# Placement in SBUF: the slots of the split-weight ring 128 bytes apart within a line of 512, other tensors moved, DMA scratch of 8 KB for 16 KB

## The reference, cut to what matters

```python
h = rms_norm(x, norm_mix)
proj, gates = h @ w_in                          # 3608 columns, then 3 x 2048 gate columns
y_a, y_b, y_c = swa(proj), stick_breaking(proj), nsa(proj)   # small attentions
merged = sum(sigmoid(g_i) * (y_i @ w_branch_i))
x = x + merged @ w_out
h = rms_norm(x, norm_ffn)
x = x + (silu(h @ w_gate) * (h @ w_up)) @ w_down
out = rms_norm(x, norm_final)
```

## Time and profile before

| | us |
|---|---|
| median of 3 runs | 1381.56 |
| fastest, slowest run | 1380.27, 1384.85 |
| span of the profiled execution (first to last instruction) | 1378.3 |
| TensorE busy, of that span | 1364.8 |
| VectorE busy | 922.5 |
| ScalarE busy | 702.5 |
| GpSimd busy | 46.2 |

### The profile page before, as it was taken

The page is one execution under the profiler, slowest core; times in us unless marked ns, Lnnn a source line. Parts: engine busy times, 40 slices in busy tenths (PEclk is TensorE's granted clock), DMA queues, the critical chain, the costliest instruction groups (busy, mean ns, idle before and its releaser), DMA issues.

```text
span 1378.3 us, 26427 instructions
## 1 busy us (share of the span) xinstructions
PE 1364.8 (99%) x11280; PEld 1332.1 (97%) x11280; DVE 922.5 (67%) x1189; ACT 702.5 (51%) x912; POOL 46.2 (3%) x70
## 2 busy tenths in 40 slices
PE   8999999999999999999999999999999999999997
PEld 8999999999999999999999999999999999999997
DVE  6455557667654657666788788875446788887554
ACT  7333356656545654465654555454334455545444
POOL 4000010000000110000000000000000000000111
PEclk9999999999999999999999999999999999999999
DMA  7777755455565767546556756566556665666653
GB/s 255 245 217 217 212 148 154 140 151 141 152 192 163 198 204 221 179 163 200 165 181 198 219 171 196 185 208 210 195 195 181 191 211 172 196 194 231 210 195 123
DMA packets 135264, 261.08 MB, mean 189 GB/s; under 512 B 8448, under 2 KB 25408, under 8 KB 134768
## 3 DMA queue, kind: packets, MB, share of 16 engines
q1 hardware_dynamic: 133328, 251.89, 59.8%
q0 software_dynamic: 1792, 7.57, 1.5%
q10 hardware_dynamic: 32, 0.01, 0.0%
HBM read 257.33 MB, written 2.10 MB: 188 GB/s over the span
## 4 chain that ended last, share of the span: by engine, by line
PE 89%; DVE 8%; ACT 1%; issue 1%; ACTq 0%; POOL 0%; DVEq 0%; POOLq 0%
PE bank L638 24%; PE bank L639 23%; PE bank L640 23%; PE bank L877 5%; PE bank L880 4%; PE bank L879 4%; PE bank L627 2%; DVE weight_lo_ring L1269 2%; DVE weight_sums_lo L1289 1%; DVE weight_sums L1278 1%; PE bank L776 1%; DVE act_rows L1329 1%; ACT weight_hi_ring L1039 1%; PE bank L687 1%; DVE raw_ring L1280 1%
## 5 line engine op out<-in xcount | busy, mean ns | idle before, releaser
L1269 DVE TENSOR_TENSOR weight_lo_ring<-raw_ring,weight_hi_ring 128x1024 fp32r<-128x1024 f32 (+2 forms) x480 | 581.0, 1220 | 317.0 <-ACT weight_hi_ring L1039 263.4
L1039 ACT ACTIVATE weight_hi_ring<-raw_ring 128x1024 fp32r<-128x1024 f32 (+2 forms) x432 | 449.1, 1052 | 348.6 <-PE bank L640 281.1
L638 PE MATMUL bank<-weight_hi_ring,hT_hi 128*128 128x256 f32 (+2 forms) x1280 | 384.5, 300 | 0.8 <-DVE weight_lo_ring L1269 0.8
L639 PE MATMUL bank<-weight_lo_ring,hT_hi 128*128 128x256 f32 (+2 forms) x1280 | 378.0, 295 | 0.0
L640 PE MATMUL bank<-weight_hi_ring,hT_lo 128*128 128x256 f32 (+2 forms) x1280 | 377.8, 295 | 0.0
L638 PEld LDWEIGHTS bank<-weight_hi_ring,hT_hi 128*128 128x128 f32 x1280 | 241.1, 188 | 12.5 <-issue 7.5
L639 PEld LDWEIGHTS bank<-weight_lo_ring,hT_hi 128*128 128x128 f32 x1280 | 240.5, 188 | 4.5
L640 PEld LDWEIGHTS bank<-weight_hi_ring,hT_lo 128*128 128x128 f32 x1280 | 240.4, 188 | 4.7
L638 PE MATMUL bank<-weight_hi_ring,h2T_hi 128*128 128x256 f32 x704 | 196.3, 279 | 2.2 <-DVE weight_lo_ring L1269 2.1
L640 PE MATMUL bank<-weight_hi_ring,h2T_lo 128*128 128x256 f32 x704 | 195.3, 277 | 0.0
L639 PE MATMUL bank<-weight_lo_ring,h2T_hi 128*128 128x256 f32 x704 | 195.2, 277 | 0.0
(11 more groups left out here) (238 smaller groups left out, 1883.2 us busy)
## 6 DMA issues: line engine op xcount, KB each, us to landing
raw_ring<-in_w_in SPq DMA_DIRECT2D x96, 512.0 KB, 3.6
raw_ring<-in_w_gate SPq DMA_DIRECT2D x88, 512.0 KB, 4.3
raw_ring<-in_w_up SPq DMA_DIRECT2D x88, 512.0 KB, 4.2
raw_ring<-in_w_down SPq DMA_DIRECT2D x88, 512.0 KB, 4.1
raw_ring<-in_w_in SPq DMA_DIRECT2D x56, 452.0 KB, 3.7
raw_ring<-in_w_out SPq DMA_DIRECT2D x32, 512.0 KB, 3.9
raw_ring<-in_w_br_c SPq DMA_DIRECT2D x16, 256.0 KB, 3.9
raw_ring<-in_w_br_a SPq DMA_DIRECT2D x16, 256.0 KB, 6.7
```

The lines of the kernel that those rows point to most:

```text
L638: pe.matmul(dst, x_hi, w_hi, start=opening, stop=False, skip_group_check=True)
L639: pe.matmul(dst, x_hi, w_lo, start=False, stop=False, skip_group_check=True)
L1039: act.activation(whi[:, s, :, 0:width(u)], raw[:, s, :, 0:width(u)], ACT.Copy).then_inc(hi_ready, 1)
L1269: dve.tensor_tensor(lo, w, hi.bitcast(F32), ALU.subtract).then_inc(lo_ready, 1)
```

## The change

The order of instructions is the same on all five engines; only addresses and the size of the scratch change, so that no row of any engine's order differs but in its line number.

- A slot of `weight_hi_ring` and of `weight_lo_ring` takes 32 elements (128 bytes) more, which nobody uses. The four hi slots then start at 128, 256, 384 and 0 past a multiple of 512 bytes (before: all at 128). `weight_lo_ring` starts at 192, so its slots are at 192, 320, 448 and 64 (before: all at 128). `raw_ring` stays at 128.
- `softmax_small` moves ahead of `x`; with the rings' growth `x` goes from 0 to 256 and `identity` from 128 to 192 past a multiple of 512.
- `h2T_hi`/`h2T_lo` move by half a line, from 192 to 448. The feed-forward tensors (`actT_*`, `silu`, `act_rows`, the products' and sums' rows, `h2_sums_*`) move by 32 bytes, from 192 to 224. `weight_sums_hi`/`_lo` stay at 128; `hT_*` and `yT_*` stay at 192.
- The DMA scratch at the foot of SBUF, which GpSimd's transfers use, has 8,192 bytes for 16,384; everything moves down by that much.

In bytes, the start of the stationary operand less that of the moving one, modulo 512, was 64 in every big product. It is now, by slot 0 to 3: `hT`, `yT` with hi 64, 448, 320, 192, with lo 0, 384, 256, 128; `h2T` with hi 320, 192, 64, 448, with lo 256, 128, 0, 384; `actT`, `h2_sums` with hi 96, 480, 352, 224, with lo 32, 416, 288, 160.

```diff
+SKEW = 32
...
+        def next_line(phase):
+            top[0] += (phase - top[0]) % LINE
+
         raw = place("raw_ring", [RING, UK, W])
-        whi = place("weight_hi_ring", [RING, UK, W], F32R)
-        wlo = place("weight_lo_ring", [RING, UK, W], F32R)
+        whi_slots = place("weight_hi_ring", [RING, UK * W + SKEW], F32R)
+        next_line(MOVING + 2 * SKEW)
+        wlo_slots = place("weight_lo_ring", [RING, UK * W + SKEW], F32R)
+        whi, wlo = ([m[:, s, 0:UK * W].rearrange("p (k c) -> p k c", k=UK) for s in range(RING)]
+                    for m in (whi_slots, wlo_slots))
...
         rstd = place("rstd", [TT])
+        small = place("softmax_small", [2, 6, 2, 2])
         X = place("x", [TT, D])
...
-        small = place("softmax_small", [2, 6, 2, 2])
...
-        h2T_hi = at("h2T_hi", [KD, S], mid, F32R)
-        h2T_lo = at("h2T_lo", [KD, S], mid + 4 * KD * S, F32R)
-        span = [low]
+        h2_at = mid + LINE // 2
+        h2T_hi = at("h2T_hi", [KD, S], h2_at, F32R)
+        h2T_lo = at("h2T_lo", [KD, S], h2_at + 4 * KD * S, F32R)
+        span = [low + SKEW]
...
-        ext_at = mid + 8 * KD * S + (MOVING - STATIONARY) % LINE
+        ext_at = mid + 8 * KD * S + LINE + (MOVING - STATIONARY) % LINE
...
-                    w_hi, w_lo = (m[:, slot, k, a:b] for m in (whi, wlo))
+                    w_hi, w_lo = (m[slot][:, k, a:b] for m in (whi, wlo))
...
-    nc = bacc.Bacc("TRN2", target_bir_lowering=False, num_devices=1)
+    nc = bacc.Bacc("TRN2", target_bir_lowering=False, num_devices=1, dynamic_dma_scratch_size=8192)
```

More of the change, by code:

```diff
@@ L258, in build_layer @@
         rstd = place("rstd", [TT])
+        small = place("softmax_small", [2, 6, 2, 2])
         X = place("x", [TT, D])
-        def next_line(phase):
-            top[0] += (phase - top[0]) % LINE
         next_line(STATIONARY)
@@ L882, in quarters @@
             def quarters(u, k, c):
-                return tuple(m[:, u % RING, k, c * Q4:(c + 1) * Q4] for m in (whi, wlo))
+                return tuple(m[u % RING][:, k, c * Q4:(c + 1) * Q4] for m in (whi, wlo))
             def up_unit(u, i, j):
@@ L1038, in split @@
                     act.wait_ge(raw_ready[s], landed(u))
-                act.activation(whi[:, s, :, 0:width(u)], raw[:, s, :, 0:width(u)], ACT.Copy).then_inc(hi_ready, 1)
+                act.activation(whi[s][:, :, 0:width(u)], raw[:, s, :, 0:width(u)], ACT.Copy).then_inc(hi_ready, 1)
             def split_in_loop(u0, rounds, units, cols=W):
@@ L1045, in split_in_loop @@
                 act.wait_ge(unit_used, units + (u0 - RING + 1))
-                act.activation(whi[:, s, :, 0:cols], raw[:, s, :, 0:cols], ACT.Copy).then_inc(hi_ready, 1)
+                act.activation(whi[s][:, :, 0:cols], raw[:, s, :, 0:cols], ACT.Copy).then_inc(hi_ready, 1)
             def hi_of_transposed(n, b, dst, gain):
@@ L1267, in split_unit @@
                 dve.wait_ge(hi_ready, count)
-                lo, w, hi = (m[:, slot, :, 0:cols] for m in (wlo, raw, whi))
+                lo, w, hi = wlo[slot][:, :, 0:cols], raw[:, slot, :, 0:cols], whi[slot][:, :, 0:cols]
                 dve.tensor_tensor(lo, w, hi.bitcast(F32), ALU.subtract).then_inc(lo_ready, 1)
```

## The result

The changed kernel takes 1412.34 us (median of four runs, 1411.0 to 1412.62) against 1381.92 of the kernel before in the same comparison (four runs, 1380.27 to 1384.85): a ratio of 1.021, with a 95% interval of 1.0187 to 1.0233. It is 30.4 us slower. Forecast were 1374 us, 1356 to 1398.

A forecast was written before the change was run, and what follows sets the result against it. TensorE's matmul pace was taken as the bound. Slow matmuls reaching the better pace gave -7.4 us, all other parts zero, so 1381.6 - 7.4 = 1374 us, range 1356 to 1398; faster 43%, same 27%, slower 30%.

The forecast's parts named there:

- What bounds the kernel: Whole kernel: TensorE busy 1364.8 of 1378.3 us at full clock; only its matmul pace, 113.3 or 117.8 ns, is left.
- no split, small tensor or scratch costs anything: ScalarE's and VectorE's splits, moved identity, x and softmax_small, and halved scratch: each priced at zero, hidden or at the floor.
- The wide matmuls: The 768 matmuls of 452 and 444 columns, at 206.7 and once 200 ns: at most 5.1 us, taken as nothing.
- the mean of both ends: Big products at unknown slot distances: mean of 109 ns floor and 117.8 slow pace, so no change for matmuls at 113.3.
- The other term, -7.4 us: Slow stretches, chiefly w_out and first gate and up products: slow matmuls reach the better pace, 4.45 ns less each.
- the 1,660 slow matmuls: Some 1,127 in three long slow stretches plus some 530 in short ones, out of 9,819 matmuls of 256 columns.
- the second, the slow pace spreading: Rival 2, 30%: all big products, most of all w_down and gates, slow at 4.45 ns a matmul; 1396 to 1418 us.
- upper end 36.3 us: Upper bound for the big products: all 9,819 matmuls at 117.8 ns, 36.3 us more.
- the middle, half of the matmuls: Rival 2's middle price: half of the 9,819 matmuls slow, 14.5 us more, 1396 us.
- the nearest row for distance: Transposes at distances 384 and 64, 108 and 110 ns: no difference beyond rounding, but bound by their loads.
- no effect at 27%: Rival 1, 27%: placement does nothing, slow stretches stay give or take 2 us; 1380 to 1383 us.
- the 4 and 16 ns of the prediction: Excess of measured 113.3 and 206.7 ns over the skill's 109.2 and 190.8 for 256 and 452 columns, called unknown to the rule.

## Why the prediction was wrong

**What bounds the kernel** was right: TensorE's pace alone, with two levels at one placement that lie 4.45 ns a matmul apart. **That no split, small tensor or scratch costs anything** was right; each was shown by a run or by the rows of the changed kernel. The wide matmuls, taken as nothing, changed by less than 1 us in the first projection.

**The step that failed** is the one at which I took the mean of both ends, "(109 + 117.8) / 2 = 113.4 ns, the steady pace of now", for slots at unknown distances. At none of thirteen distances tried did the pace come near 109 ns, and twelve had 117 to 120: the slow pace was the rule and 113.3 ns the exception. The measured mean was 117.8 ns in gates, branches, `w_out`, gate and up products, and 118.3 in `w_down`. The lo ring's offset went into this mean as one more unknown distance, with no price of its own, and it alone costs what the whole change costs.

**The other term, -7.4 us,** was the whole of the forecast gain: the 1,660 slow matmuls should drop to 113.4, because a relation that differs at each unit boundary would not hold the slow pace. They did not drop (745 matmuls for 746 in 88 us). The reason given was not what failed: with the slots apart and hi and lo alike, the good slots of `w_out` go at 113.5 ns where the kernel before held 117.8. What failed is again the pace to drop to, since no slot of the changed kernel had a good one. And the term was over-priced even so: the slow stretches come and go at one placement, and where 750 slow matmuls fell away, with the scratch alone halved, more stops took back 2.4 of 3.9 us in gate and up.

**The rival that came true** is the second, the slow pace spreading. Its price held (4.45 ns a matmul, upper end 36.3 us; the steady distances grew by 39.5 us over the four stages of 256 columns), but I gave it the middle, half of the matmuls, and cut the range at a little over half. It took all of them, less 7.8 us that came back at the pauses of gate and up, which I had not reckoned. The slots alone, two good and two bad, came to 12.7 us, near the 14.5 of that middle; the lo ring's offset and the feed-forward rows took the rest. I chose the nearest row for distance from transposes, which are bound by their loads and show nothing of a 256-column stream, and said so, and still let it keep a chance for no effect at 27%.

**Which edit did it.** The lo ring's offset of 64 bytes alone costs 32.4 us over the kernel before; slots 128 bytes apart alone 12.7; the feed-forward rows' 32 bytes 11.6 in `w_down`; h2T's half line, x, identity, scratch nothing that shows. They do not add up, since a stage that is already at 118 ns cannot be slowed by it again: slots and rows without the lo offset cost 18.2 us (1402.03 against 1383.82), and the offset the rest.

**What stays open.** Why 64 modulo 256 is good is not known, nor why one start of three at another distance takes the good pace from its neighbours, with the low stationary operands moved along or not. It was not tried to move the low stationary operands alone. What switches between 113.3 and 117.8 ns at the good distance, beyond that a pause precedes it, is not settled either. No kernel tried beats the one before.

The Trainium skill, SBUF — State Buffer, section "Who interferes with whom", gives TensorE one read port for the moving operand and an independent one for the weight load. If they were all that counts, placement could not matter; the measurement decides otherwise: TensorE is 5% slower in `w_down` by where its own two operands start, 118.7 for 113.3 ns. At which point the two reads meet, no run shows. The Trainium skill, TensorE: Matmul & The Clock Gate, section "Back-to-back issue gap", has a formula for a single matmul by itself, by which an estimate for 256 columns is 109.2 ns; no stage of 256 columns here reached it. For a stream of weight loads and matmuls, as this kernel has, the section says that both set the spacing, so the 4 and 16 ns of the prediction do not speak against it.

## What to carry to other kernels

Where TensorE is the bound and runs at full clock, read the distance between starts over a whole stage and compare stages: a steady 118 ns for 113 is worth more than every wait in this kernel. Place both operands at one distance that has been measured, keep high and low halves and all ring slots at that same distance modulo 256 (strides of 256 bytes cost nothing that could be measured here, strides of 64 or 128 did), and do not skew slots in the hope of an average. When one placement alone has been seen, an unknown one should be priced from the levels that the trace already shows as frequent outcomes after a disturbance, not from the mean of the bounds. Before a slow stretch is counted as something to win, look at a second trace of the same placement: here the longest one was not in it.

## What the runs showed of the hardware

- With a new stationary operand for every 256-column float32r matmul at a granted clock of 1.00, the level of 2.4 GHz, the pace depends on the distance of the two starts in a partition, modulo 256 bytes where that was tried (64 and 320, 32 and 288, 192 and 448): 113.3 ns at 64 and, over whole stages, 117.0 to 120.1 at twelve others, 119.9 only eight bytes away. Transposes of 128 columns kept 109 ns, matmuls of 452 columns had 206.7 ns at 64 and 204.4 at 48 and 72.
- Places shifted together by 32 bytes (1.0008, 0.9982 to 1.0034) and strides of 256 between matmuls (1.0006, 0.997 to 1.0043) cost nothing that could be measured; an offset of 64 bytes between the two moving operands that alternate costs 2.3%.
- At the good distance there are two steady paces, 113.3 and 117.8 ns. The slow one starts behind a pause and is held through hundreds of matmuls, but not across a change of distance from one unit to the next (113.5 ns in the good slots of `w_out`). At the distances scanned no 24 matmuls in a row went under 116.4 ns.
- A slower TensorE gets fewer stops: in gate and up products 17 distances between starts over 130 ns for 43, 7.8 us back; a faster one gets more, 49 and 2.4 us more, in the trace with the halved scratch.
